# The triangular inversion of an RWKV-7 layer: 64x64 blocks with masks, or packed 32x32 diagonal blocks and a corner product

## The reference, cut to what matters

```python
def step(state, inp):
    r_t, w_t, k_t, v_t, a_t, b_t = inp
    sa = jnp.einsum('bhij,bhj->bhi', state, a_t)
    state = (state * w_t[:, :, None, :] + sa[..., None] * b_t[:, :, None, :]
             + v_t[..., None] * k_t[:, :, None, :])
    return state, jnp.einsum('bhij,bhj->bhi', state, r_t)
```

## Time and profile before

| what | value |
| --- | --- |
| median of three runs | 943.93 us |
| profiled execution | 943.67 us |
| its span (first to last instruction) | 941.9 us |
| mean granted TensorE clock, as a share of the full one | 0.998 |
| TensorE matmuls | 6960, busy 926.5 us |
| VectorE | 1278, busy 682.4 us |
| ScalarE | 782, busy 482.0 us |
| GpSimd | 78, busy 102.1 us |

### The profile page before, as it was taken

How to read it: one execution, slowest core, us unless ns; L and a number is a source line. 1 busy time by engine, 2 the same in 40 slices (tenths; PEclk the granted TensorE clock), 3 DMA queues, 4 the chain that set the end, 5 groups by cost and what they waited for, 6 DMA issues and landing times.

```text
span 941.9 us, 18168 instructions
## 1 busy us (share of the span) xinstructions
PE 926.5 (98%) x6960; PEld 817.4 (87%) x6960; DVE 682.4 (72%) x1278; ACT 482.0 (51%) x782; POOL 102.1 (11%) x78
## 2 busy tenths in 40 slices
PE   9999999999999999999999999999999999999998
PEld 7779789798879888888899999999998798888887
DVE  7886886868756666666697888888878666666665
ACT  4542434324334544454457777777677454444442
POOL 0111100101011000000032133213221000000000
PEclk9999999999999999999999999999999999999999
DMA  9411212201415676676379545544553246666661
GB/s 298 152 60 46 90 59 90 94 11 50 132 45 172 188 210 182 193 200 200 105 210 292 152 133 164 157 144 137 166 157 112 69 144 192 199 200 182 192 181 46
DMA packets 195242, 136.77 MB, mean 145 GB/s; under 512 B 7390, under 2 KB 186078, under 8 KB 195052
## 3 DMA queue, kind: packets, MB, share of 16 engines
q1 hardware_dynamic: 194892, 135.71, 48.5%
q10 hardware_dynamic: 288, 0.20, 0.1%
HBM read 134.83 MB, written 1.05 MB: 144 GB/s over the span
## 4 chain that ended last, share of the span: by engine, by line
PE 89%; DVE 7%; ACT 2%; issue 1%; POOL 0%; DVEq 0%; ACTq 0%
PE bank L483 50%; PE wide L483 35%; DVE work L1455 3%; DVE work L1749 1%; ACT work L1076 1%; PE wide L1019 1%; PE bank L1019 1%; ACT L1076 1%; DVE work L1458 1%; DVE x L1455 1%; PE wide L996 0%; PE bank L996 0%; ACT Vs L1076 0%; PE bank L506 0%; POOL gsm L2044 0%
## 5 line engine op out<-in xcount | busy, mean ns | idle before, releaser
L483 PE MATMUL bank<-wpj,hkq 128*128 128x384 f32 x1152 | 215.3, 340 | 1.5 <-ACT Vs L1076 0.4
L483 PEld LDWEIGHTS bank<-wpj,hkq 128*128 128x128 f32 x1152 | 197.4, 188 | 6.1 <-issue 4.2
L483 PE MATMUL wide<-hsp,wsp 128*128 128x256 f32 (+2 forms) x1120 | 193.4, 329 | 0.0
L483 PEld LDWEIGHTS wide<-hsp,wsp 128*128 128x128 f32 x1120 | 172.4, 190 | 23.0 <-DVE hsp L1455 0.6
L1455 DVE TENSOR_TENSOR wsp<-ring,wsp 128x1024 fp32r<-128x1024 f32 (+1 forms) x88 | 150.7, 1752 | 4.2 <-ACT wsp L1076 4.2
L1076 ACT ACTIVATE wsp<-ring 128x1024 fp32r<-128x1024 f32 (+1 forms) x88 | 130.4, 1485 | 23.5 <-DMA ring<-in_f_w_gu 12.3
L2044 POOL TENSOR_TENSOR gsm<-gsm,mhalf 128x6 f32<-128x6 f32 (+1 forms) x40 | 74.3, 1876 | 264.6 <-DVE gsm L1962 173.9
L483 PE MATMUL bank<-wsp,asp 128*128 128x512 f32 x396 | 98.1, 392 | 0.0
L1455 DVE TENSOR_TENSOR wpj<-ring,wpj 128x1536 fp32r<-128x1536 f32 x48 | 84.1, 1753 | 17.0 <-ACT wpj L1076 17.0
L1076 ACT ACTIVATE rows<-wide 128x256 f32<-128x256 f32 x66 | 25.3, 383 | 115.8 <-PE wide L483 115.7
L483 PEld LDWEIGHTS bank<-wsp,asp 128*128 128x128 f32 x396 | 71.7, 189 | 13.2
(11 more groups left out here) (277 smaller groups left out, 1322.0 us busy)
## 6 DMA issues: line engine op xcount, KB each, us to landing
ring<-in_f_w_gu SPq DMA_DIRECT2D x88, 512.0 KB, 5.9
ring<-in_w_kv SPq DMA_DIRECT2D x96, 256.0 KB, 3.5
ring<-in_f_w_down SPq DMA_DIRECT2D x44, 512.0 KB, 3.7
ring<-in_b_w_q SPq DMA_DIRECT2D x48, 256.0 KB, 3.4
wmix<-in_a_w_k SPq DMA_DIRECT2D x4, 1024.0 KB, 5.5
wmix<-in_a_w_r SPq DMA_DIRECT2D x4, 1024.0 KB, 5.1
wmix<-in_a_w_v SPq DMA_DIRECT2D x4, 1024.0 KB, 5.5
wmix<-in_a_w_o SPq DMA_DIRECT2D x4, 1024.0 KB, 5.2
```

The lines of the kernel that those rows point to most:

```text
L483: return pe.matmul(o, a, b, start=start, stop=stop)
```

## The change

Up to level 4 nothing is non-zero outside the 32x32 diagonal blocks of U. The change packs the four of them for each unit (P x 8 x 32) in place of the two 64x64 blocks, and works on 32x32 tiles of the array, at four places on its diagonal. Levels 1 to 4 run with masks as before, on half the elements. Level 5, from 32 to 64, becomes a corner product: for each pair of blocks one 32x32 product with M's corner, a copy without a mask, and one with U, which VectorE copies to Us. The diagonal 32x32 blocks of Us are copied by ScalarE in four instructions, which TensorE and GpSimd wait for (`act_Ud`). GpSimd zeroes all of Us at the start. The table of constants has five masks of 32 columns in place of six of 64, and `eye4` of 32 columns added.

```diff
+QB = 32
...
         Us = cg.take(8 * P, "p (u t) -> p u t", u=8)
-        Uc = cg.take(8 * HD, "p (u t) -> p u t", u=8)
+        Uc = cg.take(8 * QB, "p (u t) -> p u t", u=8)
+        Tq = cg.take(8 * QB, "p (u t) -> p u t", u=8)
         Tc = cg.take(8 * HD, "p (u t) -> p u t", u=8)
         over_X = cg.take(8 * P)
+        Xq = over_X[:, 0:8 * QB].rearrange("p (u t) -> p u t", u=8)
...
+        QUARTERS = [slice(b * QB, (b + 1) * QB) for b in range(P // QB)]
+        PAIRS = ((QUARTERS[0], QUARTERS[1]), (QUARTERS[2], QUARTERS[3]))
...
+                def quarter(b, u):
+                    return b[:, u % 4 * QB:(u % 4 + 1) * QB]
+
                 for l in range(1, LEVELS - 1):
+                    corner = l == LEVELS - 2
...
                         for u in range(4 * q, 4 * q + 4):
-                            for hb in BLK:
-                                m = mm(bank[q][hb, u % 4 * HD:(u % 4 + 1) * HD], M[hb, u, 0, hb], Tc[hb, u, :])
+                            for i, o in PAIRS if corner else zip(QUARTERS, QUARTERS):
+                                m = mm(quarter(bank[q], u)[o, :], M[i, u, 0, o], Tq[i, u, :])
                         m.then_inc(S("pe_X"), 1)
...
                         for u in range(4 * q, 4 * q + 4):
-                            for hb in BLK:
-                                m = mm(bank[2 + q][hb, u % 4 * HD:(u % 4 + 1) * HD], Xc[hb, u, :], Uc[hb, u, :])
+                            for o, i in PAIRS if corner else zip(QUARTERS, QUARTERS):
+                                m = mm(quarter(bank[2 + q], u)[o, :], Xq[i, u, :], Uc[i, u, :])
                         m.then_inc(S("pe_U"), 1)
                     values_fill(l)
 
                 lo, up = BLK
                 pe.wait_ge(S("act_g"), it + 1)
                 pe.wait_ge(S("act_kn"), it + 1)
+                pe.wait_ge(S("act_Ud"), it + 1)
...
                 A(Vn.rearrange("p c n i -> p (c n i)"), bank[6], ACT.Copy).then_inc(S("act_vn"), 1)
+                act.wait_ge(S("dve_U"), it * 12 + 10)
+                for b in QUARTERS:
+                    m = A(Us[b, :, b], Uc[b, :, :], ACT.Copy)
+                m.then_inc(S("act_Ud"), 1)
                 act.wait_ge(S("pe_z0"), it + 1)
...
-                    for hb in BLK:
-                        m = dve.copy_predicated(Uc[hb, us, :], first_level[hb, 0:1, :].broadcast_to([HD, 4, HD]), M[hb, us, 0, hb])
+                    for b in QUARTERS:
+                        m = dve.copy_predicated(Uc[b, us, :], first_level[b, 0:1, :].broadcast_to([QB, 4, QB]), M[b, us, 0, b])
...
-                        tt(Xc[:, us, :], bank[h][:, 0:256].rearrange("p (u t) -> p u t", u=4),
-                           levels[:, l:l + 1, :].broadcast_to([P, 4, HD]), ALU.mult).then_inc(S("dve_X"), 1)
+                        new = bank[h][:, 0:P].rearrange("p (u t) -> p u t", u=4)
+                        if l < LEVELS - 2:
+                            tt(Xq[:, us, :], new, levels[:, l:l + 1, :].broadcast_to([P, 4, QB]), ALU.mult).then_inc(S("dve_X"), 1)
+                        else:
+                            dve.tensor_copy(Xq[:, us, :], new).then_inc(S("dve_X"), 1)
...
-                        new = bank[2 + h][:, 0:256].rearrange("p (u t) -> p u t", u=4)
+                        new = bank[2 + h][:, 0:P].rearrange("p (u t) -> p u t", u=4)
...
-                            for hb in BLK:
-                                m = tt(Us[hb, us, hb], new[hb], Uc[hb, us, :], ALU.add)
+                            for o, i in PAIRS:
+                                m = dve.tensor_copy(Us[o, us, i], new[o])
                             m.then_inc(S("dve_U"), 1)
...
-            pool.memset(Us[HD:P, :, 0:HD], 0.0).then_inc(S("pool_zeros"), 1)
+            pool.memset(Us[:, :, :], 0.0).then_inc(S("pool_zeros"), 1)
...
-            pool.tensor_copy(Uc, eye2).then_inc(S("pool_eye"), 1)
+            pool.tensor_copy(Uc, eye4).then_inc(S("pool_eye"), 1)
...
                     pool.wait_ge(S("dve_U"), it * 12 + 12)
-                    pool.tensor_copy(Uc, eye2).then_inc(S("pool_eye"), 1)
+                    pool.wait_ge(S("act_Ud"), it + 1)
+                    pool.tensor_copy(Uc, eye4).then_inc(S("pool_eye"), 1)
```

More of the change, by code:

```diff
@@ L53, in constants @@
     lev[0] = lev[0].T
-    out["levels"] = np.concatenate([m[:, 0:HD] + m[:, HD:P] for m in lev[:LEVELS - 1]], 1)
+    out["levels"] = np.concatenate([sum(m[:, b * QB:(b + 1) * QB] for b in range(P // QB)) for m in lev[:LEVELS - 2]], 1)
     out["eye2"] = np.concatenate([(p % HD == f[:, 0:HD])], 1).astype(np.float32)
+    out["eye4"] = (p % QB == f[:, 0:QB]).astype(np.float32)
     for r in range(RT):
@@ L220, in program @@
         tri = C("tri").bitcast(I32).rearrange("p (m t) -> p m t", m=4)
-        first_level = C("levels").bitcast(I32).rearrange("p (l t) -> p l t", l=LEVELS - 1)
-        levels = C("levels").rearrange("p (l t) -> p l t", l=LEVELS - 1)
+        first_level = C("levels").bitcast(I32).rearrange("p (l t) -> p l t", l=LEVELS - 2)
+        levels = C("levels").rearrange("p (l t) -> p l t", l=LEVELS - 2)
         BLK = (slice(0, HD), slice(HD, P))
+        QUARTERS = [slice(b * QB, (b + 1) * QB) for b in range(P // QB)]
+        PAIRS = ((QUARTERS[0], QUARTERS[1]), (QUARTERS[2], QUARTERS[3]))
         NGRP = D // 256
@@ L1748, in turn_blocks @@
                 def turn_blocks(h):
-                    dve.transpose(Tc[:, 4 * h:4 * h + 4, :].rearrange("p u t -> p (u t)"),
+                    dve.transpose(Tq[:, 4 * h:4 * h + 4, :].rearrange("p u t -> p (u t)"),
                                   Uc[:, 4 * h:4 * h + 4, :].rearrange("p u t -> p (u t)")).then_inc(S("dve_T"), 1)
@@ L2055, in _ @@
             pool.wait_ge(S("pool_zeros"), 1)
-            pool.memset(Us[HD:P, :, 0:HD], 0.0).then_inc(S("pool_zeros"), 1)
+            pool.memset(Us[:, :, :], 0.0).then_inc(S("pool_zeros"), 1)
             pool.wait_ge(S("pool_zeros"), 2)
-            eye2 = C("eye2").rearrange("p (o t) -> p o t", o=1).broadcast_to([P, 8, HD])
+            eye4 = C("eye4").rearrange("p (o t) -> p o t", o=1).broadcast_to([P, 8, QB])
             pool.wait_ge(s_const, 16)
-            pool.tensor_copy(Uc, eye2).then_inc(S("pool_eye"), 1)
+            pool.tensor_copy(Uc, eye4).then_inc(S("pool_eye"), 1)
             for it in range(NGRP):
```

## The result

The changed kernel takes **959.45 us** (median of 4 runs, 959.01 to 960.91) beside 943.92 (943.85 to 943.95, 4 runs) of the kernel before: a ratio of 1.0174, 95% interval 1.0161 to 1.0186 (the two medians alone give 1.0165). The forecast was 940.1 us with a range of 928 to 945. The profiled execution took 959.01 us around a span of 957.3, with a mean granted clock of 0.978; before it was 0.998.

A forecast was written before the change was run, and what follows sets the result against it. TensorE, busy 98% of the span, was taken as the bound, with VectorE steps on the inversion's path. Gains of 0.52 + 0.06 + 0.43 = 1.01 us a group, 4.0 in four, less 0.2 gave 940.1 us, range 928 to 945.

The forecast's parts named there:

- the clock: Rival: in the inversion's small-tile work the granted clock falls to 1.2 GHz, 3 to 4 us a group, 955; chance 0.05.
- issue rival: Rival: inversion passes limited by instruction issue at 15 ns each, or only two tiles pair: 966.7 us; chance 0.11.
- p: Time of one set of four 32x32 matmuls in an inversion pass of eight sets: 58 ns, range 56 to 63.
- columns rival: Rival: short inversion matmuls are paid by their columns, p = 32, 3.8 us a group more, 928.8 us; chance 0.25.
- VectorE's shorter steps: Inversion, halved elements: 0.13 us off each X, U addition and transpose; 0.52 us a group from X at levels 1 to 4.
- forecast 0.43: Level 5, 129.26 to 132.90: 3.64 us become 3.21 as a corner product, a gain of 0.43 us a group.
- the transpose that I had called early enough: Level 5: VectorE's last transpose, which the second pass A waits for today, would come early enough after the change.
- The predicated copies: First level: four of 128 elements for two of 256, 1.2 us for 0.91; 0.2 us lost once, in group 0.
- The cover of 0.3 us: First level, groups 1 to 3: the transpose behind the predicated copies ends before its reader starts, 0.3 us to spare.
- ScalarE's copies: Four diagonal copies into Us, ended near 131.1 before TensorE's wait: cost nothing; 1.2 us a group without that cover.
- GpSimd and the table: GpSimd's larger memset of Us, about 0.9 us, and the constant table, 192 columns smaller: cost nothing.

The follow-up runs named there:

- e7: The kernel before with one of the two 64x64 tiles in all five levels, half the result left out: 948.57 us, ratio 1.0062.
- e1: The kernel before with each 64x64 matmul of the five levels split into two of 32 moving columns: 972.8 us, ratio 1.0317.
- e2: The changed kernel with two of the four 32x32 tiles at levels 1 to 4, the other blocks' products left out: 938.06 us, ratio 0.9929.
- e3: The changed kernel with dense 128x128 matmuls, results unread, in TensorE's gaps at each level: median 963.56 us.
- e6: e4 with twelve 32x32 matmuls in each of four places, three in level 5 and one in level 4: 956.36 us, ratio 1.0153.
- e4: The kernel before with only level 5 changed to the 32x32 corner product with ScalarE's diagonal copies: 949.74 us, ratio 1.0079.
- e8: The kernel before with two of four units in level 5's passes, the others left out, gaps as long as the corner's: 941.52 us, ratio 0.9985.

## Why the prediction was wrong

**The step that failed is the clock**, the rival that had a chance of 0.05 and 955 us. The prediction dismissed it with the 1.00 in the earlier trace rows, since levels 4 and 5 "have little else than half-array work". That row shows that half of the array is enough; it says nothing of a quarter, and in level 5, where the prediction counts "four of sixteen" tiles, only two work, an eighth. e7 halves the tiles in a kernel that otherwise stays as it is, and the clock falls in 5 of 8 runs. The rival's mechanism was right (it falls in level 5 of groups 1 to 3, and the dense work behind pays), its price was not quite: 0, 5.0, 2.0 and 4.5 us behind the groups where I had 3 to 4 for each, some 16 in all with what is paid inside the inversions, the largest single term of the result. The rival's 955 us was the nearest to the measured time in part by luck: it knew neither of the breaks nor of the gain.

**The second failed step is the issue rival's mechanism.** It had instructions limited to 15 ns each, p up to 117 and the time at 966.7. Within a pass that rate doesn't exist: a pass goes at 0.30 us for 64 instructions, 4.7 ns each. What exists is a supply of program: in group 1 the trace has pieces of 256 instructions coming in from 116.6, 120.1, 124.8, 128.5 and 132.0 us on, in this kernel never closer than 3.4, which is 13.4 ns an instruction. Only over several pieces in a row does the rival's 15 come near. Passes of 58 ns a pair use a piece in 256 x 14.7 = 3.8 us; those of the changed kernel in 1.2. So the queue runs dry within a run of passes, and the breaks that have a row of their own are 2.65 us in group 0, 1.30 and 0.66 in group 1, 1.51 and 0.67 in group 2, 2.06, 0.70 and 0.51 in group 3: 10.1 us. From one start to the next they are 11.6 us, since the rows leave out the 0.19 us in which the matmul ahead is still in the array; two more of 0.28 us have no row (one of them makes the pass at 121.93 take 0.75 us for 32 instructions in place of 0.45): 12.2 us in all.

e1 (14.5 ns an instruction, no break) and e2 (half the instructions, no break, 3.5 us less in group 1's inversion) bear this out. So does the place of the breaks. The traces of the changed kernel, e3 and e6 have 24 of them with a row over 0.3 us; each stands 193 or 194 instructions past a multiple of 256, counted over all that the trace lists for TensorE, and ends 1.2 to 1.6 us after a piece has landed. The inversions of the other kernels have none. No run slowed or sped the supply alone.

**The term p was mis-sized: 58 ns forecast, 31 to 37 measured.** I took it from the rows with 1 and 14 columns, which don't get below 60, and from a pair's 58; e1 shows that the 58 don't go by the moving columns. I also leaned on the Trainium skill (TensorEngine Tiling, Instruction Overhead): by its 60 cycles, an estimate of 25 ns at 2.4 GHz, a matmul of 32 columns costs as much as one of 60. e1 agrees, where halved moving columns alone bring nothing, and a set of 31 to 37 ns lies above those 25, if its four matmuls run side by side. What failed is my use of it: the change halves the stationary columns too, and the set got shorter. The columns rival (p = 32, 3.8 us a group) was right in size: 3.58 in e2. In the changed kernel 0.10 is left of it in group 1: 2.6 us went in its three breaks, from start to start, 0.44 in level 5 (3.17 us for e2's 2.73), over which the clock falls, and most of the rest in passes that are a little longer on four tiles than on e2's two (1.33 us for 1.27, three passes).

**VectorE's shorter steps came as forecast:** X at 286 ns, U additions 291 and 277, transposes 312, for my 0.29, 0.26 and 0.32. Level 5 shrank by 0.47 in the changed kernel (131.69 to 134.86) and by 0.62 in e4, for the forecast 0.43: about right. The forecast was on the low side since its p of 58 was too high, and in e4 TensorE now waits 0.35 us there for the transpose that I had called early enough.

**The predicated copies failed as a term:** "1.2 us by slope" measured 2.02. The cover of 0.3 us was gone, and TensorE waits 0.65 us in each of groups 1 to 3 and 1.45 in place of 0.65 in group 0: 2.8 us, where I had 0.2. I extrapolated a slope of another instruction. A 64x256 copy had a row, and nothing in the trace told how its time depends on its size; that had to be bounded by "no cheaper at all", which would have opened the cover.

**Nothing for ScalarE's copies** held in the changed kernel: 1.68 us at 132.29, over at 133.97 ahead of z0's copy at 134.97, and no wait at the transposes. GpSimd and the table were free too, as put.

The sum, told afterwards, in us: some 14 of gain (3.58 a group, less in group 0), against 12.2 of breaks, some 16 of clock and the 0.5 ahead of group 0. That is some 15 of loss where 17.0 were measured; VectorE's 2.8 are already within the 3.58, which e2 has too. The 2 that are missing I can't divide; the passes on four tiles and the price of the clock, known to 0.02 or so a us, are the likely places.

## What to carry to other kernels

A smaller tile takes its gain from the same thing that endangers it: less of the array works, and TensorE's clock can fall, with most of the bill in the dense work behind. Ask for each stretch how much of the array the change leaves at work, and compare granted clocks over several runs before times. A kernel can have falls of its own elsewhere; follow one matmul of both traces through the whole program before you put a difference of spans down to the change. Count instructions per us as well: where a run of matmuls goes through 256 loads and matmuls faster than the program arrives, TensorE stands still with no semaphore to show for it.

## What was not expected of the hardware

- Matmuls and loads of 32x32 on four tiles ran at 4.7 ns an instruction, but the program came in pieces of 256 at 3.4 us or more apart: breaks of 0.5 to 2.7 us within a pass, all at the same place in the count of 256.
- TensorE busy for 98% of the time with one 64x64 tile (e7) had falls of the clock in 5 of 8 runs; with two tiles and gaps (e8) the mean clocks of 10 runs were those of the kernel before (0.996 to 1.000).
- 1 us at 1.2 GHz cost 0.40 us of time behind groups 1 and 2, and 0.45 in the kernel before's own fall (1.54 us for 3.4), not 0.5. Why the rest isn't lost was not tested.
- A pair of 64x64 matmuls cost 58 ns with 64 moving columns and with 32 (e1), a set of four 32x32 ones 31 to 37.
- COPY_PREDICATED took 489 ns for 32x128 and 496 for 64x256.
